# Moving 96 vector-weight tiles out of a four-slot weight ring: places of their own, filled by two other queue positions

## The reference, cut to what matters

```
def ada_params(cond, w, b):
    mod = jax.nn.silu(cond) @ w + b
    return jnp.split(mod, 3, axis=-1)
...
def first_block(x, ...):                 # depth 1
    h = rms_norm(x, mix_norm_g); proj = h @ w_in
    attn = mla_group(...)                # 8 heads, causal
    rec = rglru_group(...)               # gated linear recurrence
    x = x + concat(rms_norm(attn), rms_norm(rec)) @ w_out
    x = x + peer_ffn(rms_norm(x), ...)   # 256 tokens x 128 gathered rows of peer_u, and of peer_v
...
def second_block(x, c, ctx, c_ctx, ada_w, ada_b, ...):
    # layer 0: shift, scale, gate for the latent rows (c) and for the context rows (c_ctx)
    xm = x * (1 + sc) + sh
    y = mLSTM and pooling of xm @ w_in_even, keys and values of the context in front
    x = layer_norm(ALPHA * x + g * (y @ w_out_even))
    # layer 1: x @ w_in_odd, a gated spatial mixer, w_out_odd
```

## Time and profile before

| | us |
|---|---|
| median of 3 runs | 2820.23 |
| lowest, highest | 2811.22, 2820.95 |
| profiled execution | 2811.51 |
| its span in the trace | 2809.7 |

### The profile page before, as it was taken

One profiled execution on the slowest core, in us unless ns is written; L12 is line 12 of the kernel. 1 busy time (PEld: TensorE's weight loads), 2 busy tenths in 40 slices (PEclk: granted clock), 3 DMA queues, 4 the chain that ended last, 5 costly groups with the idle time before them and its releaser, 6 DMA issues.

```text
span 2809.7 us, 20509 instructions
## 1 busy us (share of the span) xinstructions
PE 1957.0 (70%) x7600; PEld 1339.8 (48%) x7600; DVE 1991.1 (71%) x2461; ACT 561.3 (20%) x804; POOL 1019.0 (36%) x600
## 2 busy tenths in 40 slices
PE   6989898969201777777776000039899898799987
PEld 3748446855000222222222000039788777688865
DVE  6866775887898666444445999988664878666566
ACT  2043200010000000010000000023434343445432
POOL 0001000353587565554554888820066540000000
PEclk9989999989655999999999555569999999899998
DMA  7763585999999999999999999967744467587632
GB/s 278 283 234 120 214 320 201 385 400 421 422 409 422 421 421 422 422 422 421 421 422 422 422 422 422 422 268 282 276 148 145 140 253 286 217 293 287 213 137 103
DMA packets 123507, 887.56 MB, mean 316 GB/s; under 512 B 13840, under 2 KB 14352, under 8 KB 16528
## 3 DMA queue, kind: packets, MB, share of 16 engines
q0 software_dynamic: 73728, 536.90, 46.0%
q1 hardware_dynamic: 45792, 325.87, 31.3%
q10 hardware_dynamic: 3888, 23.49, 2.1%
HBM read 884.11 MB, written 2.10 MB: 315 GB/s over the span
## 4 chain that ended last, share of the span: by engine, by line
PE 41%; DMA 27%; POOL 14%; DVE 12%; issue 4%; ACT 1%; SPq 0%; DVEq 0%; ACTq 0%
PE psum L699 23%; DMA W<-in_peer_v,W 15%; POOL W L573 9%; PE psum L665 7%; POOL early_rows L573 6%; PE psum L641 4%; DMA early_rows<-in_peer_v,W 3%; PE psum L871 3%; DMA early_rows<-in_peer_u,W 3%; DMA W<-in_peer_u,W 3%; DMA ring<-in_ada 1%; PE psum L916 1%; DMA ring<-in_w_out 1%; DVE ring L1556 1%; DVE split L1570 1%
## 5 line engine op out<-in xcount | busy, mean ns | idle before, releaser
L699 PE MATMUL psum<-split,hi 128*128 128x512 f32 x1664 | 522.0, 395 | 27.0 <-DVE split L1570 19.7
L1895 DVE CUSTOM_DVE_ANT_0 W<-W,XN 128x2048 f32<-128x2048 f32 x150 | 340.7, 2291 | 215.3 <-DMA W<-in_peer_u,W 214.5
L871 PE MATMUL psum<-W,HT 128*128 128x512 f32 x624 | 287.4, 604 | 281.1 <-ACT HT L1275 182.3
L1075 ACT ACTIVATE split<-ring 128x1024 fp32r<-128x1024 f32 x272 | 283.1, 1057 | 426.1 <-PE psum L699 331.0
L699 PEld LDWEIGHTS psum<-split,hi 128*128 128x128 f32 x1664 | 317.0, 191 | 94.8 <-issue 24.3
L1570 DVE TENSOR_TENSOR split<-ring,split 128x1024 fp32r<-128x1024 f32 x208 | 250.6, 1223 | 151.7 <-ACT split L1075 150.9
L573 POOL DMA_INDIRECT W<-in_peer_u,W x150 | 217.6, 1450 | 367.4 <-DVEq L1877 235.0
L1895 DVE CUSTOM_DVE_ANT_0 early_rows<-early_rows,XN 128x2048 f32<-128x2048 f32 x106 | 241.0, 2291 | 137.5 <-DMA early_rows<-in_peer_u,W 136.3
L573 POOL DMA_INDIRECT W<-in_peer_v,W x154 | 277.3, 1801 | 165.0 <-PE psum L871 136.2
L871 PEld LDWEIGHTS psum<-W,HT 128*128 128x128 f32 x624 | 112.9, 190 | 455.6 <-issue 309.2
L665 PE MATMUL psum<-HT,ring 128*128 128x256 f32 x1280 | 289.4, 390 | 42.3 <-ACT HT L1239 22.3
(11 more groups left out here) (317 smaller groups left out, 2806.8 us busy)
## 6 DMA issues: line engine op xcount, KB each, us to landing
ring<-in_ada SPq DMA_DIRECT2D x96, 1024.0 KB
ring<-in_odd SPq DMA_DIRECT2D x48, 1024.0 KB
ring<-in_w_out SPq DMA_DIRECT2D x16, 1024.0 KB
ring<-in_pq SPq DMA_DIRECT2D x16, 1024.0 KB
ring<-in_c_k SPq DMA_DIRECT2D x16, 1024.0 KB
ring<-in_c_v SPq DMA_DIRECT2D x16, 1024.0 KB
ring<-in_w_even SPq DMA_DIRECT2D x16, 1024.0 KB
ring<-in_w_odd SPq DMA_DIRECT2D x16, 1024.0 KB
```

What stands on the lines that cost most here:

```text
L699: m = nc.tensor.matmul(dst, lhs, rhs, start=(k == 0 and b == 0 and not (features and i % 2)), stop=(k == KD - 1 and b == 2 and not (featur ...
L871: m = nc.tensor.matmul(o[c], DIAG[j % DIAGS], row[:, 512 * c:512 * c + 512], start=(j == 0), stop=(j == P - 1))
L1075: A(split[:, 2048 * (n % PIECES):2048 * (n % PIECES) + 1024], ring[:, at:at + 1024], ACT.Copy)\
L1895: V.tensor_tensor_reduce(out=row, in0=row, in1=xn3[:, tt, :], scale=1.0, scalar=0.0, op0=ALU.mult, op1=ALU.add, accum_out=PACT[:, c:c + 1])\
```

## The change

Matrix weights keep the ring for themselves; no tile of `ada_w` goes through it any more. The dots stay where they were in DVE's stream, with one exception (the first chunk of `w_even` now has them behind slots 1, 2 and 3, no longer 0, 1 and 2).

The first 48 tiles are loaded by POOL's stream into two places in turn, `ADA_PLACE`: a quarter of `early_rows` (even tiles) and the lower half of `XN` (odd tiles; from tile 42 on the quarter that held the second condition row). Tile n waits for the dots of tile n - 2. The loads of tiles 0 to 24 stand ahead of POOL's three multiplications of the recurrence, the others behind them and ahead of the gathers. Tile 25 waits for the last attention score, since `XN` holds attention's operands.

The last 48 tiles have one place at a time, `ADA_LATE`, and are loaded by SP's stream: tile n's load waits for the dot of tile n - 1. It stands behind the ring load that takes the slot of the previous dot.

```
-ADA_AT = {("in_q", 0): (1, 1, 1, 1), ("in_kv", 0): (1, 1, 1, 1), ("in_x", 0): (1, 1, 1, 1), ("in_x", 1): (1, 1, 1, 1),
...
+ADA_FIRST = {"in": 8, "in_x0": 4, "in_x1": 4, "ukv": 8, "w_out0": 5, "w_out1": 5, "w_out2": 5, "w_out3": 3, "pq": 6}
+ADA_LAT, ADA_EVEN, ADA_ODD = 48, 68, 80
...
-    ADA_AT["w_even", _c] = (1, 1, 1, 0)
+    ADA_AT["w_even", _c] = (1, 1, 1, 0) if _c else (0, 1, 1, 1)
...
+    def ada_dots(self, name, c, s):
+
+        for _ in range(ADA_AT.get((name, c), NO_ADA)[s]):
             self.ada += 1
-            self.slot["ada", n] = len(self.loads)
-            self.loads.append(("ada", n, 0, 2048))
-            self.release.append((("ada_dot", ada_dots_until(n + 1)),))
+            if self.ada not in (ADA_EVEN, ADA_ODD, len(ADA_SEQ)):
+                self.ada_load.setdefault(self.slot[name, c, s] + RING, []).append(self.ada)
...
+        ADA_PLACE = [EARLY_ROWS[:, 4096:6144], XN[:, 0:2048]]
+        ADA_LATE = [XN[:, 0:2048], XN[:, 2048:4096], w(8192, 2048)]
...
+                for a in plan.ada_load.get(n, ()):
+                    sp.wait_ge(sem("ada_dot"), ada_dots_until(a))
+                    if a == ADA_LAT:
+                        sp.wait_ge(sem("dots_ready"), 3)
+                    if a == ADA_EVEN:
+                        wait_unit(sp, ("yT", 7))
...
+                    ada_load(sp, a)
...
+            def ada_loads(first, last):
+
+                for n in range(first, last):
+                    if n >= 2:
+                        pool.wait_ge(sem("ada_dot"), ada_dots_until(n - 1))
+                    if n == 1:
+                        wait_unit(pool, ("xT", 7))
+                    if n == 25:
+                        wait_unit(pool, ("score", 2 * NH - 1))
+                    ada_load(pool, n)
+
+            ada_loads(0, 25)
...
+            ada_loads(25, ADA_LAT)
```

More of the change, by code:

```diff
@@ L76 @@
 ADA_SEQ += [(1, _k, False) for _k in range(48)]
-ADA_AT = {("in_q", 0): (1, 1, 1, 1), ("in_kv", 0): (1, 1, 1, 1), ("in_x", 0): (1, 1, 1, 1), ("in_x", 1): (1, 1, 1, 1),
-          ("ukv", 3): (8,),
-          ("w_out", 0): (1, 1, 1, 2), ("w_out", 1): (1, 1, 2, 1), ("w_out", 2): (1, 1, 1, 2), ("w_out", 3): (1, 1, 1, 0),
-          (("pq", 0), 0): (2, 2, 1, 1)}
+ADA_FIRST = {"in": 8, "in_x0": 4, "in_x1": 4, "ukv": 8, "w_out0": 5, "w_out1": 5, "w_out2": 5, "w_out3": 3, "pq": 6}
+ADA_LAT, ADA_EVEN, ADA_ODD = 48, 68, 80
+ADA_AT = {}
 for _step in (("l_q", 0), ("l_q", 1), ("l_k", 0), ("l_k", 1), ("l_v", 0), ("l_v", 1)):
@@ L136, in __init__ @@
         self.unit, self.slot, self.release, self.loads = {}, {}, [], []
-        self.used = self.piece_used = self.ada = 0
+        self.used = self.piece_used = 0
+        self.ada, self.ada_load = ADA_LAT, {}
         self.lo = {"dve": 0, "pool": 0}
@@ L161, in gemm_chunk @@
                 self.release.append((self.full(self.unit[name, (c + 1) * units - 1]),))
-            self.ada_slots(ADA_AT.get((name, c), NO_ADA)[s])
     def full(self, u):
         return f"bank_full{u % BANKS}", u // BANKS + 1
-    def ada_slots(self, count):
-        for _ in range(count):
-            n = self.ada
+    def ada_dots(self, name, c, s):
+        for _ in range(ADA_AT.get((name, c), NO_ADA)[s]):
             self.ada += 1
-            self.slot["ada", n] = len(self.loads)
-            self.loads.append(("ada", n, 0, 2048))
-            self.release.append((("ada_dot", ada_dots_until(n + 1)),))
+            if self.ada not in (ADA_EVEN, ADA_ODD, len(ADA_SEQ)):
+                self.ada_load.setdefault(self.slot[name, c, s] + RING, []).append(self.ada)
     def split_chunk(self, name, c, units):
@@ L189, in split_chunk @@
                 self.release.append(tuple(("lo_" + e, count) for e, count in self.piece_lo[-2:]))
-                self.ada_slots(ADA_AT.get((name, c), NO_ADA)[j // 2])
+                self.ada_dots(name, c, j // 2)
             if j < 7:
@@ L244, in make_plan @@
             p.gemm("l_g", 1, 1, 1, 256)
+            p.ada_dots("l_g", 0, 0)
         else:
@@ L272, in make_plan @@
     assert p.ada == len(ADA_SEQ)
+    for n, step in ((ADA_LAT, ("l_q", 0, 3)), (ADA_EVEN, ("w_even", 0, 3)), (ADA_ODD, ("odd", 0, 3))):
+        p.ada_load.setdefault(p.slot[step], []).append(n)
     return p
@@ L474, in build, with ada_place, ada_load @@
         COND_JUNK = EARLY_ROWS[:, 2048:4096]
+        ADA_PLACE = [EARLY_ROWS[:, 4096:6144], XN[:, 0:2048]]
+        ADA_LATE = [XN[:, 0:2048], XN[:, 2048:4096], w(8192, 2048)]
         COND_LAT = [XN[:, 2048:4096], XN[:, 0:2048], w(10240, 2048)]
         ADA0_DOTS, ADA1_DOTS, GATE1_DOTS = ada_dots_until(48), ada_dots_until(80), ada_dots_until(96)
+        def ada_place(n):
+            if n < ADA_LAT:
+                place = COND1[1] if n % 2 and n >= 42 else ADA_PLACE[n % 2]
+                return place, sem(f"ada_full{n % 2}"), 16 * (n // 2 + 1)
+            return ADA_LATE[(n >= ADA_EVEN) + (n >= ADA_ODD)], sem("ada_late"), 16 * (n - ADA_LAT + 1)
+        def ada_load(eng, n):
+            l, k, _ = ADA_SEQ[n]
+            place, full, _ = ada_place(n)
+            eng.dma_start(place, t["ada"][l, k]).then_inc(full, 16)
         def bank(key):
@@ L524, in _ @@
                         sp.wait_ge(sem(name_), value)
[L525 to L528, removed]
+                if isinstance(name, tuple):
                     src = t[name[0]][name[1], s]
@@ L533, in _ @@
                 sp.dma_start(ring[:, 2048 * slot:2048 * slot + width], src).then_inc(sem(f"slot_full{slot}"), 16)
+                for a in plan.ada_load.get(n, ()):
[4 more added lines that the diff above has]
+                        wait_unit(sp, ("yT", 7))
+                    if a == ADA_ODD:
+                        for eng in ("act", "pool", "dve"):
+                            sp.wait_ge(turned("x3T", eng), turned_before["x3T"] + 4)
+                    ada_load(sp, a)
             for n in range(2 * TT):
@@ L1378, in _ @@
             A(GROWS[0:8, 0:2, 0:S], GROWS[0:8, 0:2, S:2 * S], ACT.Exp, scale=-1.0).then_inc(sem("rows_ready"), 1)
+            act.wait_ge(sem("ada_dot"), ada_dots_until(ADA_EVEN))
             latent_hi("l_u", 1, l_u)
@@ L1548, in ada_dots @@
                     l, k, dual = ADA_SEQ[n]
[L1549 to L1552, removed]
+                    w_, full, value = ada_place(n)
+                    dve.wait_ge(full, value)
+                    rows = COND1 if n < ADA_LAT else [COND_LAT[(n >= ADA_EVEN) + (n >= ADA_ODD)]]
                     if dual and n:
@@ L1616, in _ @@
             dve.wait_ge(sem("cond_ready"), 2)
-            ada_dots(8)
+            ada_dots(ADA_FIRST["in"])
             dve.wait_ge(sem("c_raw"), 4)
@@ L1628, in _ @@
                 if i % 2 == 0:
-                    ada_dots(4)
+                    ada_dots(ADA_FIRST[f"in_x{i // 2}"])
                 wait_unit(dve, ("in_x", i))
@@ L1658, in _ @@
                 m.then_inc(sem("xc_ready"), 1)
-            ada_dots(8)
+            ada_dots(ADA_FIRST["ukv"])
             dve.wait_ge(sem("hg_loaded"), 16)
@@ L1787, in _ @@
                 if i % 2 == 0:
-                    ada_dots(sum(ADA_AT["w_out", i // 2]))
+                    ada_dots(ADA_FIRST[f"w_out{i // 2}"])
                 wait_unit(dve, ("w_out", i))
@@ L1814, in _ @@
             dve.wait_ge(sem("fn_ready"), 2 * 4)
-            ada_dots(sum(ADA_AT[("pq", 0), 0]))
+            ada_dots(ADA_FIRST["pq"])
             issued = [0]
```

## The result

The change made the kernel slower, by 1%. In the same rounds the median was 2848.3 us (2841.2 to 2854.0, 4 runs) against 2820.6 us (2811.2 to 2822.4, 4 runs) of the kernel before; the ratio is 1.0104, 95% interval 1.007 to 1.0137. The forecast was 2822 with a range to 2842. The profiled execution of the changed kernel took 2841.2 us (span 2839.4), 29.7 more than that of before.

The account below looks back on a forecast made before the run. PE bounds both blocks (waiting for ring loads in the first), DMA the gathers. Terms -27.5 + 2.5 + 19.7 + 12 = +6.7 give 2818.2 us from the profiled 2811.5, 2826.9 from the median; forecast 2822, range 2803 to 2842.

Parts of the forecast that it names:

- Part 1: First block: without ada tiles in the ring, PE's ring-load waits go, 25.1 us plus 7.9 of clock, less 2.4 at start: 30.6.
- The 10.5 us ahead of `in_y`: First block: PE's wait for ring loads before in_y, behind eight ada tiles filling the ring, expected to go.
- The term of `in_kv` and `in_x`: First block: ring-load waits of 1.0 and 5.7 us expected to go, with clock given back behind such stops.
- I take 27.5, nearer to the lower L, because the gather's 8.05 had company: First block: gain chosen between 30.6 and about 18 us, for POOL load times L from 5.9 to about 8 us.
- The higher L: First block: POOL load time of about 8 us, from the first gather's 8.05; in_kv, in_x and w_out gains then lost.
- POOL's loads are slow: Rival, first block: loads of 8 us and more, gain only 12 to 18, total +19, 2831 us; chance 0.22.
- for w_out the 18 tiles end at 409 or 424: First block: DVE's w_out tiles end at 409 or 424 us, depending on POOL's load time, against 417 before.
- the 421 of the prediction: First block, w_out: time in us at which PE could end; with 8 us loads the 4.1 us gain is lost.
- Part 2: First block: two places filled by POOL, each taking 4.6 us plus load time for two tiles; block gains 27.5 us.
- Part 3: Gathers: SP loads one MB more during them, at 422 GB/s, costing +2.5 us.
- Part 4: Latent chunks: one place makes dot to dot 7.2 us against 6.1; four chunks +8.4, with l_g and l_v +19.7 us.
- Part 5: w_even: one place makes DVE's chunk 25.6 us against PE's 21.9 to 22.3; three chunks, +12 us taken.

## Why the prediction was wrong

**Part 1, start to `in_y`'s end** (-21 forecast, -15.4 measured). The 10.5 us ahead of `in_y` went, and its clock came back: from PE's start of `uq` to the end of `in_y` the kernel before took 111.9 us and the changed one 98.5, 13.4 less where 13.5 had been summed. The term of `in_kv` and `in_x` failed: -2.0 at the start of `uq` where 6.7 + 1.5 + 1.7 - 2.4 = 7.5 had been summed. PE ended `in_x` at 134.2, as forecast, but DVE's last dot of it was done at about 140, not 132, and PE then stood 10.6 us.

**The step that failed** is "I take 27.5, nearer to the lower L, because the gather's 8.05 had company". The loads had company too: with the ring four weights ahead, 37 of POOL's 48 loads had over 0.5 MB beside them. The higher L was the right end: 7.0 to 7.4 measured, 5.0 to 5.4 with little beside it, 5.5 to 5.7 with half the ring's bytes. Taken with that L in place of 5.9, a pair of tiles takes 11.9 us and not 10.5, and DVE is behind PE. The rival "POOL's loads are slow" named the consequence, DVE behind PE at the 16th tile, and priced the block at -12 to -18; -18.6 came without attention and -11.8 with it. I gave it 0.22.

**Part 1, attention** (0 forecast, +6.8 measured). Two things that the prediction doesn't have. PE's first scores start 11.9 us behind the end of `in_y` and not 9.5: DVE's recurrence, which had 9.7 us to spare, now ends behind `in_y`, and the copies that the scores read stand behind it. The six profiles with two places in the first block have 11.3 to 12.2 there, the other six 9.5, so these 2.4 us are the change's. The other 4.4 can't be put down to it: from the first scores to `w_out` the profile of before took 38.9 us, with the full clock for at least 30 of them, and the other two with the same first block took 43.4 and 50.3; those with two places 43.3 to 51.8. That stretch at full clock is, as far as the second profile of the same kernel shows, also why the profiled execution of before lay 8.7 under the median, which I had seen but not placed.

**Part 1, `w_out` and `pq`** (-9.6 forecast, -3.2 measured). The ring waits went, but the evacuations stand behind 18 tiles that came too slowly: "for w_out the 18 tiles end at 409 or 424", in the times of the kernel before; they ended at 418, with `w_out` begun 8.6 us earlier than before, so at 427 in those times. PE was done at 412, which is the 421 of the prediction. The upper end of L was again the nearer, and still too low.

**Part 2, POOL's stream.** That the loads ahead of POOL's first multiplication are not on the path was right: PE's waits don't name it. POOL's issues took 0.53 us each in the changed kernel, at most 0.72, 14 of the 48 beside a dot, and not the 0.94 of a gather's issue that I had taken. If the lock that the Trainium skill tells of, SBUF — State Buffer, "Who interferes with whom", held for an issue beside a dot, some would have stood for a whole dot of 2.3 us; none of the 48 did. The same section of the Trainium skill says that a DVE instruction with two inputs in SBUF contends with a GpSimd instruction that reads SBUF and not with one that only writes.

**Part 3, gathers** (+2.5, measured +2.1): right.

**Part 4, latent chunks** (+19.7, measured +24.3). From the last gather to the gates' end it took 132.8 us in place of 123.7, +9.1 for the 8.4 of the sum, and `l_v` 0's slots came within 0.4 us of the times given. Mis-sized was `l_v` 1, where two dots waited 4.25 and 2.6 us and not about 1. It has no convolutions to hide a load under, so that with 4.8 us of load a dot waits 2.6, and the first of the two loads ran beside a ring load and took 6.5. The run with tile 61's load moved shows that this position alone was 12 us.

**Part 5, `w_even`** (+12, measured +14.7). A chunk took 26.7 us, not 25.6. The chain of the changed kernel shows the loads, of which the first of a chunk stands beside a ring load:

```profile
2354.85 2.36 DVE split L1607 x2
2357.21 2.26 DVE XN L1593
2359.51 5.82 DMA XN<-in_ada
2365.35 2.35 DVE XN L1593
2367.74 4.84 DMA XN<-in_ada
```

The same mistake as in part 1, smaller: 4.8 us is a load with little beside it.

The misses are 5.6, 6.8 and 6.4 us ahead of the gathers, less the 3.1 by which I had taken part 1 lower than its terms, 15.7 in all; 4.6, 2.7 and 0.5 behind the gathers, less 0.4 in them: 23, the distance from +6.7 to +29.7. The range ended at 2842 because its upper end took -15 us ahead of the gathers and +34 for parts 4 and 5, where -11.8 and +39.0 came. Loads in company are behind both, so the dear ends of the parts come together; 4.4 of attention's 6.8 us lie beside that, in the spread of the execution.

## What to carry to other kernels

Price a moved load with the company that it will have after the change: where the change lets another stream run further ahead, the loads beside it are longer than any row of a load alone. A place of its own for a stream is worth having only if there are enough places: two here lost half of the gain in the first block, and one place behind the gathers, with the load between two uses in full, lost all of it and more. Three places in front and two behind gave 1.6%. And before a load is put into a queue, see what the entry ahead of it waits for; a position one entry earlier was worth 12 us.

## What the runs showed of the hardware

POOL's queue took 5.1 us from issue to landing for 1 MB with little beside it, SP's 4.8; in the first block a lone one took 5.0 to 5.4, and in the company of a second stream of 1 MB loads they took 7.0 to 7.4, and with three places in flight 7.7 to 8.1.

TensorE's clock in a stretch of small dependent products, with PE busy 7 to 10 us of 10, was granted at 2.4 GHz in one execution and at 1.2 GHz for thirty microseconds in another of the same program. The stretch is 11 us longer then, as much as the whole spread of the kernel's runs (2811 to 2822 us); that the others of its runs differ for this reason is not shown. A profile of one execution should be compared with another over the stages without such a stretch.
